# A two-layer trunk with mixture-of-experts on one core: two more experts in the fixed order, the order product and the id reads moved, the layer ends reordered

## The chip, the cores and the metric

One core of a Trainium2 chip runs the whole program. The metric is the device time of one execution in microseconds (us). All data are float32 unless a line says bf16. The profile is one execution taken by the hardware profiler; its times count from the start of its span.

## The reference, cut to what matters

Two layers work on 256 tokens (128 of a context pass, 128 of a denoising step) with 1024 columns. Each layer is a mixer followed by a mixture of experts; the change touches the mixture and the two places behind it.

```python
def hier_moe(h, w_rg, b_rg, w_re, b_re, w_g, w_u, w_d):      # h: tokens x 1024
    g_prob = softmax(x @ w_rg + b_rg)                        # 4 groups
    p_group, g_idx = top_k(g_prob, 1)
    e_in = the 8 expert logits of the chosen group
    top_p, top_i = top_k(softmax(e_in), 2)                   # 2 of 32 experts per token
    wts = top_p / sum(top_p) * p_group
    hid = silu(x @ w_g[e]) * (x @ w_u[e])                    # w_g, w_u: 1024 x 256 each
    y   = sum over e of gate[e] * (hid @ w_d[e])             # w_d: 256 x 1024
```

After each mixture `x = x + g2 * y`; after layer 0 the next mixer begins with a root mean square norm of `x`, after layer 1 the final norm `rms_norm(x, final_norm)` is the output. An expert has three matrices of 1 MiB, so the 32 experts of a layer are 96 MiB, and each of them is read once per layer. For the inputs given, the reference's routing sends these numbers of tokens to the experts that the kernel treats as fixed: layer 0, experts 0 to 7: 15, 22, 29, 16, 12, 7, 11, 24; layer 1: 31, 12, 18, 24, 12, 32, 10, 23. The four largest of the other 24 are 34, 34, 26, 23 in layer 0 and 71, 45, 44, 35 in layer 1.

## The kernel before, in words

**Routing.** `moe(l)` on each engine makes the router's logits, the masks and, by products with a triangle, the place of each token within its expert (`pos`) and the gates (`gat`). The experts 0 to 5 (`NFIX = 6`) are handled in a fixed order; the other 26 are ranked by how many tokens they have, so that an expert with many tokens gets many places. `order_by_count` on VectorE computes the ranks, and `order_tables` on TensorE turns them into ids with a small product (the order product, line L1319). VectorE's `ordered` writes the ids as integers into `route_i` (L2435) and SyncE reads them into registers.

**Passes.** The mixture runs in 11 passes, q = 0 to 10 (`PASSES`). Each pass fills the 128 columns of one tile of tokens: a pair has two experts with 64 places each, a quad four with 32, mono one with 128, and "three" one with 64 and two with 32. Pass by pass TensorE does: the up products (gate and up matrices of the pass, L1343, or by halves of the 1024 rows, L1357), the scatter of the pass before (L1400), transposes (`turn`), the gather of the next pass's tokens in two halves (L1333), the down products (L1389). ScalarE and VectorE copy the halves of the gather into `xg` (semaphores `m_xg1`, `m_xg0`) and apply the activation. In the last pass the down products and the scatter are cut in two (`last_down`, L1371, and `scatter_last`, L1407).

**Weights.** SyncE issues all weight transfers in one order into 11 slots of 2 MiB (`RING + MORE`). An up slot holds gate and up of one expert (or, by halves, half the rows of two experts); a down slot holds the down matrices of two experts, or of one alone where the pass has an odd number. A pass takes `slots_of(q)` slots: n for the ups and (n + 1) // 2 for the downs. Numbered in the order of the stream, slot p of a layer reuses the place of slot p - 11, and `slot_free(c)` waits on the semaphore `used` until TensorE has finished with that one (for the first slots of a layer with chunks of the work ahead: slots 9 and 10 come free by the modulation chunks 10 and 11 that `moe(l)` works through, L860). The ups of a pass give their slots back when the up products are done (by halves: half by half), the downs when the down products are. SyncE waits for the ids before pass 3, reads all ids of a pass and then issues its transfers:

```python
if q == NFIX // 2:
    sp.wait_ge(S.v_pos, 3 * l + 3)
```

**Layer ends.** After the last pass TensorE scatters the second half once VectorE's `weighted_rows` has written it (L2469). Then each engine reads the number of overflow rounds (`moe_further`; with more tokens than places an expert gets further rounds) and branches; the else side is empty. VectorE then adds the result to `xT` in four blocks (`add_scaled`, L2348) and, after layer 1, multiplies by the final gain into `hT` (L2614). ScalarE squares each block. After layer 1 TensorE transposes the first half into rows (`rows_out(0)`, L1558), sums the squares (L1566), and transposes the second half; the two row halves are scaled and stored.

Of the kernel before, what the change touches and what calls it, by code (L numbers as in the profile page):

```python
# [27 lines left out]
NB = 2  # L28
# [16 lines left out]
NFIX = 6  # L45
# [21 lines left out]
TILES = ([(NRANK + e, j) for e in range(NFIX) for j in range(2)] + [(r, j) for r in range(RANK4) for j in range(4)]  # L67
         + [(r, j) for r in range(RANK4, RANK2) for j in range(2)] + [(r, 0) for r in range(RANK2, NRANK)])
SHARE = {"mono": [0], "pair": [0, 1], "three": [0, 0, 1, 2], "quad": [0, 1, 2, 3]}
# [248 lines left out]
def build(nc, I, O):  # L318
    ctx = ExitStack()
    with ctx:  # L320
# [119 lines left out]
        sqo = part(4096, (KT, T))  # L440
# [63 lines left out]
        sqf = part(14100, (KT, T))  # L504
# [154 lines left out]
        def _(sp):  # L659
# [40 lines left out]
            def moe_layer(l):  # L700
                for q in range(NPASS):
                    c = moe_at[l] + PASS_AT[q]
                    if q == NFIX // 2:
                        sp.wait_ge(S.v_pos, 3 * l + 3)
                    ids = []
                    for kind, e in PASSES[q][1]:
                        if kind == "r":
                            e = sp.value_load(route_i[0:1, l, 9 + e:10 + e], min_val=0, max_val=NE - 1)
                        ids.append(e)
                    if by_halves(q):  # L710
# [5 lines left out]
                    else:  # L716
                        for e in ids:
                            expert_up(l, c, e)
                            c += 1
# [104 lines left out]
        def _(pe):  # L824
# [522 lines left out]
            def up_by_halves(share, c, between=None):  # L1347
# [63 lines left out]
            def moe_experts(l):  # L1411
# [4 lines left out]
                gather(1, 0, S.m_gat)  # L1416
                order_tables(l)
# [1257 lines left out]
```

## Time and profile before

| | |
|---|---|
| time of the kernel, median of 3 runs | 843.94 us (842.47 to 844.89) |
| the profiled execution's own time | 846.4 us |
| its span | 844.6 us |
| TensorE busy | 789.3 us, 93% of the span |
| VectorE, ScalarE busy | 321.8 us, 166.8 us |
| mean granted TensorE clock | 0.973 |
| moved by DMA | 291.47 MB, mean 345 GB/s |

The busy share of TensorE is an average over stages with different limits; the rate of the DMA over time says more here. The two mixtures lie at about 279 to 496 us (layer 0) and 616 to 832 us (layer 1).

### The profile page before, as it was taken

What the parts mean: (1) busy time and instruction counts of PE and PEld (TensorE: products, weight loads), DVE (VectorE), ACT (ScalarE), POOL (GpSimd) and SP (SyncE); (2) the same over time, 40 slices, a digit from 0 to 9 for tenths busy, and PEclk for the clock granted to TensorE, in tenths of its full rate; (3) what the DMA queues carried; (4) which work ended last, traced back from release to release, by engine and by line L of the source; (5) the groups of instructions that cost most, each with busy time, mean ns of one, the idle gap of its engine ahead of it and who ended that gap; (6) DMA issues with size and microseconds to landing.
All of it is one profiled execution on the core that took longest, in us unless ns stands there. A gap on an engine that the chain in (4) does not pass through costs nothing.

```text
span 844.6 us, 15977 instructions
## 1 busy us (share of the span) xinstructions
PE 789.3 (93%) x6913; PEld 525.5 (62%) x6913; DVE 321.8 (38%) x687; ACT 166.8 (20%) x323; POOL 12.3 (1%) x17
## 2 busy tenths in 40 slices
PE   3999999998999999999986989989999999999787
PEld 3788568677798665456542444779865555644335
DVE  1155467653414433433332340241543443333224
ACT  3112411323203111111110141130311111111012
POOL 0000001020000000000000000000000000000000
PEclk9999999999999999999998999999999999999898
DMA  9999779493899299999999999996549999999991
GB/s 342 387 371 386 260 261 349 147 345 108 270 393 395 111 417 410 402 416 415 420 414 412 401 386 385 388 409 269 199 168 416 407 398 417 415 421 416 410 398 70
DMA packets 97879, 291.47 MB, mean 345 GB/s; under 512 B 11833, under 2 KB 14991, under 8 KB 87567
## 3 DMA queue, kind: packets, MB, share of 16 engines
q1 hardware_dynamic: 86960, 284.32, 86.5%
q10 hardware_dynamic: 10847, 6.11, 2.5%
q8 instruction: 56, 0.92, 0.4%
q14 instruction: 16, 0.13, 0.0%
HBM read 288.30 MB, written 2.10 MB: 344 GB/s over the span
## 4 chain that ended last, share of the span: by engine, by line
PE 70%; SPq 11%; DMA 11%; ACT 3%; DVE 3%; issue 2%; ACTq 1%; DVEq 0%
PE psum L1357 7%; PE psum L1264 7%; PE psum L907 7%; PE psum L1343 5%; PE psum L1333 5%; PE psum L967 5%; DMA ring<-in_w_exp_up 5%; DMA scratch<-in_w_exp_up 5%; PE psum L860 5%; SPq L744 5%; PE psum L1389 4%; PE psum L1515 3%; PE psum L1528 3%; PE psum L1400 3%; SPq L733 2%
## 5 line engine op out<-in xcount | busy, mean ns | idle before, releaser
L1343 PE MATMUL psum<-scratch,hT 128*32 128x512 f32 (+1 forms) x384 | 79.5, 659 | 15.1 <-DMA ring<-in_w_exp_up 8.6
L1333 PE MATMUL psum<-scratch 128*128 128x128 f32 x704 | 84.0, 279 | 0.9 <-DVE scratch L2460 0.9
L1333 PEld LDWEIGHTS psum<-scratch 128*128 128x128 f32 x704 | 82.0, 195 | 1.2 <-issue 1.2
L1343 PE MATMUL psum<-ring,hT 128*32 128x512 f32 (+1 forms) x288 | 69.9, 641 | 2.5 <-DMA scratch<-in_w_exp_up 2.5
L907 PE MATMUL psum<-hT,ring 128*128 128x256 f32 x256 | 57.8, 382 | 1.1 <-DVE hT L2051 0.7
L1400 PEld LDWEIGHTS psum<-const,scratch 128*128 128x128 bf16 x480 | 45.1, 97 | 21.5 <-issue 13.6
L1400 PE MATMUL psum<-const,scratch 128*128 128x256 bf16 x480 | 55.9, 272 | 1.5 <-DVE scratch L2476 1.5
L2469 DVE TENSOR_SCALAR hT<-psum,const 128x512 f32<-128x512 f32 x22 | 16.5, 751 | 106.3 <-PE psum L1389 93.6
L1343 PEld LDWEIGHTS psum<-scratch,hT 128*32 128x32 f32 (+1 forms) x384 | 21.4, 123 | 54.5 <-issue 54.5
L907 PEld LDWEIGHTS psum<-hT,ring 128*128 128x128 f32 x256 | 47.8, 190 | 9.6 <-DVE hT L2051 2.0
L1885 ACT ACTIVATE scratch<-psum 128x256 f32<-128x256 f32 x22 | 8.5, 384 | 210.0 <-PE psum L1343 123.2
L1357 PE MATMUL psum<-scratch,hT 128*64 128x512 f32 (+1 forms) x208 | 42.7, 593 | 0.3 <-DMA scratch<-in_w_exp_up 0.3
L967 PE MATMUL psum<-ring,hT 128*128 128x512 f32 x96 | 42.6, 596 | 0.0
L860 PE MATMUL psum<-ring,condT 128*2 128x128 f32 x1280 | 40.1, 280 | 1.0 <-issue 1.0
L2480 DVE TENSOR_TENSOR scratch<-psum,scratch 128x256 f32<-128x256 f32 x22 | 9.3, 425 | 83.0 <-ACT scratch L1885 82.9
L1389 PE MATMUL psum<-scratch,const 128*32 128x512 f32 (+2 forms) x248 | 40.1, 596 | 0.0
L860 PEld LDWEIGHTS psum<-ring,condT 128*2 128x2 f32 x1280 | 32.2, 87 | 8.5 <-issue 5.3
L1357 PE MATMUL psum<-ring,hT 128*64 128x512 f32 (+1 forms) x176 | 35.7, 594 | 1.3 <-DMA ring<-in_w_exp_up 1.3
L1343 PEld LDWEIGHTS psum<-ring,hT 128*32 128x32 f32 (+1 forms) x288 | 18.2, 121 | 27.5 <-issue 27.5
L1389 PE MATMUL psum<-ring,const 128*32 128x512 f32 (+2 forms) x216 | 32.8, 596 | 0.0
L967 PEld LDWEIGHTS psum<-ring,hT 128*128 128x128 f32 x96 | 17.8, 190 | 20.8 <-issue 20.8
L1264 PEld LDWEIGHTS psum<-hT,ring 128*128 128x128 f32 x256 | 28.8, 192 | 0.7 <-issue 0.7
(334 smaller groups left out, 1032.8 us busy)
## 6 DMA issues: line engine op xcount, KB each, us to landing
ring<-in_w_mod SPq DMA_DIRECT2D x40, 1024.0 KB, 11.4
scratch<-in_w_exp_down SPq DMA_DIRECT2D x28, 1024.0 KB, 16.2
ring<-in_w_exp_down SPq DMA_DIRECT2D x24, 1024.0 KB, 17.4
scratch<-in_w_exp_gate SPq DMA_DIRECT2D x22, 1024.0 KB, 16.8
scratch<-in_w_exp_up SPq DMA_DIRECT2D x22, 1024.0 KB, 18.4
ring<-in_w_exp_gate SPq DMA_DIRECT2D x18, 1024.0 KB, 15.5
ring<-in_w_exp_up SPq DMA_DIRECT2D x18, 1024.0 KB, 18.2
scratch<-in_w_exp_gate SPq DMA_DIRECT2D x26, 512.0 KB, 11.0
```

The source lines that it names most:

```text
L744: sp.dma_start(slot(s)[:, at:at + 1024], w[e][:, 1024 * kh:1024 * kh + 1024]).then_inc(full[s], 16)
L860: last = mm(bank[mbank[g]][32 * m:32 * m + NB, at:at + P], condT[:, :, k], w[:, k, m * P:(m + 1) * P], start=(k == 0), stop=(k == KT - 1))
L907: last = mm(out[:, c2 * T:(c2 + 1) * T], w[:, k, m * P:(m + 1) * P], hT[:, k, :, :], start=(k == 0 and k1 == KT), stop=(k == k1 - 1), skip ...
L967: last = mm(bank[b], hT[:, k, t, :], w[:, k, :], start=(k == 0), stop=(k == KT - 1))
L1264: last = mm(bank[2 * t + m // 4][:, (m % 4) * P:(m % 4 + 1) * P], w[m // 4][:, k, (m % 4) * P:(m % 4 + 1) * P], hT[:, k, t, :], start=(k = ...
L1333: last = mm(bank[b][:, k * P:(k + 1) * P], hrow[:, t, half * 4 + k, :], Pm[:, t, :], start=(t == 0), stop=(t == 1))
L1343: last = mm(bank[0][i * m:(i + 1) * m, :], xg[:, k, i * m:(i + 1) * m], w[e][:, k, :, :], start=(k == 0), stop=(k == KT - 1))
L1357: last = mm(bank[0][i * m:(i + 1) * m, :], xg[:, 4 * kh + k, i * m:(i + 1) * m], w[i // 2][:, i % 2, k, :, :], start=(kh == 0 and k == 0), ...
L1389: last = mm(bank[1 + half][i * m:(i + 1) * m, :], hidT[:, a, i * m:(i + 1) * m], slot(slots[e // 2])[:, base:base + 512], start=(a == 0), ...
L1400: last = mm(bank[4 + k // 2][:, (k % 2) * T:(k % 2 + 1) * T], y3[:, j, k, :], ohT, start=False, stop=True, skip_group_check=True)
L1515: last = mm(bank[4 + 2 * j + t], hT[:, k, t, :], w[:, k, :], start=(k == 0), stop=(k == KT - 1))
L1528: last = mm(bank[b][:, (m % 2) * T:(m % 2 + 1) * T], w[:, k, m * P:(m + 1) * P], hT[:, k, :, :], start=(k == 0), stop=(k == KT - 1))
```

## The change

1. Passes: `NFIX` goes from 6 to 8. Experts 6 and 7 get 32 places each and share a new pass 3, a "three", with the expert of rank 3 (64 places). The quads move back; the last pass stays a quad of ranks.
2. SyncE waits for the ids at the first ranked expert of pass 3 only, which is now that pass's third, and reads each id just before that expert's transfer (passes that are not by halves).
3. TensorE: the order product stands between the two halves of the first gather; the second half goes to bank 4 instead of bank 0; the four transposes of `pos` and `gat` follow it (`rows_of_tables`), with a count of their own on `t_pos`. VectorE's `ordered` goes ahead of `weighted`. The first pass's up products wait only for the half of `xg` that they read.
4. Layer ends: `scatter_last(1)`, `weighted_rows` and the additions move into both sides of the branch. On the else side the first block is added before `weighted_rows`; after layer 1 the sums of squares are made block by block (`square_sums`), the first ahead of `scatter_last(1)`, and the final gains of the first half go to a place of their own (`finl`). The squares of layer 0's end go to `sqm` as well.

```diff
-NFIX = 6
+NFIX = 8
+NPAIR = 3
...
-          ("quad", [("r", 6 + i) for i in range(4)], 24), ("pair", [("r", 1), ("r", 2)], 16),
-          ("quad", [("r", 10 + i) for i in range(4)], 28), ("mono", [("r", 0)], 12),
-          ("quad", [("r", 14 + i) for i in range(4)], 32), ("quad", [("r", 18 + i) for i in range(4)], 36),
-          ("three", [("r", 3), ("r", 4), ("r", 5)], 20), ("quad", [("r", 22 + i) for i in range(4)], 40)]
+          ("three", [("e", 6), ("e", 7), ("r", 3)], 20), ("quad", [("r", 4 + i) for i in range(4)], 24),
+          ("pair", [("r", 1), ("r", 2)], 16), ("quad", [("r", 8 + i) for i in range(4)], 28), ("mono", [("r", 0)], 12),
+          ("quad", [("r", 12 + i) for i in range(4)], 32), ("quad", [("r", 16 + i) for i in range(4)], 36),
+          ("quad", [("r", 20 + i) for i in range(4)], 40)]
...
-SHARE = {"mono": [0], "pair": [0, 1], "three": [0, 0, 1, 2], "quad": [0, 1, 2, 3]}
+SHARE = {"mono": [0], "pair": [0, 1], "three": [0, 1, 2, 2], "quad": [0, 1, 2, 3]}
...
             def moe_layer(l):
                 for q in range(NPASS):
                     c = moe_at[l] + PASS_AT[q]
-                    if q == NFIX // 2:
-                        sp.wait_ge(S.v_pos, 3 * l + 3)
                     ids = []
                     for kind, e in PASSES[q][1]:
                         if kind == "r":
+                            if q == NPAIR:
+                                sp.wait_ge(S.v_pos, 3 * l + 3)
                             e = sp.value_load(route_i[0:1, l, 9 + e:10 + e], min_val=0, max_val=NE - 1)
                         ids.append(e)
+                        if not by_halves(q):
+                            expert_up(l, c, e)
+                            c += 1
...
-            def order_tables(l):
+            def rows_of_tables(l):
 
                 for n, v in enumerate((pos, gat)):
                     for t in range(NB):
-                        nc.tensor.transpose(bank[1][0:NE, (2 * n + t) * P:(2 * n + t + 1) * P], v[:, t, 0:NE], ident)
+                        last = nc.tensor.transpose(bank[1][0:NE, (2 * n + t) * P:(2 * n + t + 1) * P], v[:, t, 0:NE], ident)
+                last.then_inc(S.t_pos, 1)
+
+            def order_tables(l):
+
                 pe.wait_ge(S.v_pos, 3 * l + 2)
...
                 for kh in range(2):
+                    pe.wait_ge([S.m_xg0, S.m_xg1][kh], n_pass + 1)
                     for u in range(c + n * kh, c + n * kh + n):
                         slot_full(pe, u)
...
                 pe.wait_ge(S.v_pos, 3 * l + 1)
-                gather(1, 0, S.m_gat)
                 order_tables(l)
+                gather(1, 4, S.m_gat)
+                rows_of_tables(l)
...
-                        idle_products(3, 3)
-                        pe.wait_ge(S.m_yr1, n + 1)
-                        scatter_last(1).then_inc(S.t_fin, 1)
...
+            def square_sums(b):
+
+                pe.wait_ge(S.a_sq, SQ0[5] + b + 1)
+                for k in (2 * b, 2 * b + 1):
+                    for t in range(NB):
+                        last = mm(bank[t][:, 0:1], sqm[:, k, t * P:(t + 1) * P], ones[:, 0:1],
+                                  start=(k == 0), stop=(k == KT - 1), skip_group_check=True)
+                return last
...
                 with pe.Else():
-                    pe.nop()
+                    if l == DEPTH - 1:
+                        square_sums(0)
+                    else:
+                        idle_products(3, 3)
+                    pe.wait_ge(S.m_yr1, (l + 1) * NPASS)
+                    scatter_last(1).then_inc(S.t_fin, 1)
...
+            square_sums(1)
             rows_out(0)
-            for k in range(KT):
-                if k % 2 == 0:
-                    pe.wait_ge(S.a_sq, SQ0[5] + k // 2 + 1)
-                for t in range(NB):
-                    last = mm(bank[t][:, 0:1], sqf[:, k, t * P:(t + 1) * P], ones[:, 0:1],
-                              start=(k == 0), stop=(k == KT - 1), skip_group_check=True)
-            last.then_inc(S.t_ms, 1)
+            square_sums(2)
+            square_sums(3).then_inc(S.t_ms, 1)
             rows_out(1)
...
                         V.tensor_copy(xg[:, 0:4, :], heads(bank[3])).then_inc(S.m_xg0, 1)
+                        ordered(l)
                         weighted(gat[:, :, 0:2], 2).then_inc(S.m_p, 1)
-                        ordered(l)
                         overflow(l)
...
                 with dve.Else():
-                    dve.nop()
-
-                for b in range(4):
-                    dve.wait_ge(S.t_fin, 2 * l + 1 + b // 2)
-                    add_scaled(bank[4 + b], b, l * MT + 5 * KT).then_inc(S.v_y, 1)
+                    add_experts(l, 0)
+                    dve.wait_ge(S.used, done)
+                    weighted_rows().then_inc(S.m_yr1, 1)
+                    add_experts(l, 1)
                     if l == DEPTH - 1:
...
+                        final_weights(0)
+                        final_weights(1)
+                    add_experts(l, 2)
+                    add_experts(l, 3)
+                    if l == DEPTH - 1:
+                        final_weights(2)
+                        final_weights(3)
```

## Rows read from the trace of the kernel before

**Rows 1.** The page's GB/s of DMA, in 40 slices of 21.1 us.
```profile
GB/s 342 387 371 386 260 261 349 147 345 108 270 393 395 111 417 410 402 416 415 420 414 412 401 386 385 388 409 269 199 168 416 407 398 417 415 421 416 410 398 70
```
**Rows 2.** Windows: stretch, its length, TensorE's clock, DMA busy share, GB/s.
```profile
273.70:290.10 16.40, 0.90 0.06 15
290.10:345.40 55.30, 1.00 1.01 412
345.40:346.60 1.20, 1.00 0.78 212
346.60:480.20 133.60, 0.96 1.02 414
...
601.00:625.00 24.00, 0.93 0.24 89
...
681.80:816.10 134.30, 0.96 1.02 414
```
**Rows 3.** Waits of SyncE's queue, 280 to 500 us: total, times, longest.
```profile
SPq L708 <- DVE route_i L2435: 22.9, 1, 22.9
```
**Rows 4.** Timeline of SyncE's issues, layer 0: start, us, line, transfer, count.
```profile
262.08 0.89 SPq L763 DMA_DIRECT2D ring<-in_w_exp_down  x2
288.54 0.37 SPq L733 DMA_DIRECT2D ring<-in_w_exp_gate  x1
...
345.05 0.33 SPq L733 DMA_DIRECT2D ring<-in_w_exp_gate  x1
```
**Rows 5.** Pieces of the chain that ended last: start, us, what.
```profile
273.06 3.91 PE psum L860 x127
...
279.36 5.44 PE psum L1333 x32
285.70 7.02 PE psum L1357 x32
...
302.50 6.87 PE psum L1357 x32
...
337.85 7.00 PE psum L1343 x64
...
426.70 8.80 PE psum L1343 x64
```
**Rows 6.** Timeline of VectorE: the ids of layer 0 are written.
```profile
285.74 0.17 DVE L2435 CAST route_i<-psum 1x26 int32<-1x26 f32 x1 [2.60 <-PE psum L1320]
```
**Rows 7.** TensorE timeline: up products behind a wait (in brackets, with its releaser).
```profile
452.17 1.06 PE L1343 MATMUL psum<-scratch,hT 128*32 128x512 f32 x2 [6.39 <-DMA ring<-in_w_exp_up]
...
480.39 3.64 PE L1357 MATMUL psum<-scratch,hT 128*32 128x512 f32 x32 [0.26 <-DMA scratch<-in_w_exp_up]
...
816.25 3.64 PE L1357 MATMUL psum<-ring,hT 128*32 128x512 f32 x32 [1.30 <-DMA ring<-in_w_exp_up]
```
**Rows 8.** TensorE windows: length, busy (instructions), granted clock, DMA share, GB/s.
```profile
424.30:426.70 2.40, 0.00 (x0) 1.00 0.99 401
...
427.20:430.40 3.20, 3.20 (x21) 0.51 1.03 410
...
837.00:838.00 1.00, 1.00 (x6) 0.50 0.00 0
```
**Rows 9.** Timeline of VectorE and TensorE at the two layer ends.
```profile
494.07 4.23 DVE L2348 SCALAR_TENSOR_TENSOR xT<-psum,modT,xT 128x128 f32<-128x128 f32 x16
...
829.05 0.75 DVE L2469 TENSOR_SCALAR hT<-psum,const 128x512 f32<-128x512 f32 x1 [6.37 <-PE psum L1371]
829.91 1.13 DVE L2348 SCALAR_TENSOR_TENSOR xT<-psum,modT,xT 128x128 f32<-128x128 f32 x4
831.07 0.62 DVE L2614 TENSOR_SCALAR hT<-xT,cols 128x256 f32<-128x256 f32 x2
...
834.36 4.53 PE L1566 MATMUL psum<-const,scratch 128*128 128x1 f32 x32
...
834.98 1.12 DVE L2348 SCALAR_TENSOR_TENSOR xT<-psum,modT,xT 128x128 f32<-128x128 f32 x4
```

More of the change, by code:

```diff
@@ L439, in build @@
         vtk = part(2048, (NB, D))
-        sqo = part(4096, (KT, T))
         vsq = part(6144, (D,))
@@ L503, in build @@
         yrow = part(12000, (NB, D))
-        sqf = part(14100, (KT, T))
+        finl = part(2304, (4, NB, P))
         ab = small[:, 0:32]
@@ L715, in moe_layer @@
                                 c += 1
[L716 to L719, printed above, removed]
                     if q == NPASS - 1:
@@ L1345, in experts_up, with up_by_halves @@
                 last.then_inc(sem, n)
-            def up_by_halves(share, c, between=None):
+            def up_by_halves(share, c, n_pass, between=None):
                 n = len(share) // 2
@@ L1557, in rows_out @@
                     for k in range(4):
[L1558 removed]
+                        last = nc.tensor.transpose(bank[2 + 2 * t + half][:, k * P:(k + 1) * P],
+                                                   finl[:, k, t, :] if half == 0 else hT[:, 4 + k, t, :], ident)
                     last.then_inc(S.t_last, 1)
+            square_sums(1)
             rows_out(0)
[L1562 to L1568 removed]
+            square_sums(2)
+            square_sums(3).then_inc(S.t_ms, 1)
             rows_out(1)
@@ L1935, in _ @@
             roots()
[L1936 removed]
+            stream_squares(3, sqm)
             norm(3, 1, 1, 0)
@@ L2563, in moe_experts @@
                         V.tensor_copy(xg[:, 0:4, :], heads(bank[3])).then_inc(S.m_xg0, 1)
-                    dve.wait_ge(S.used, c + sum(slots_of(q)))
                     if more:
+                        dve.wait_ge(S.used, c + sum(slots_of(q)))
                         weighted_rows().then_inc(S.m_v, 1)
@@ L2604, in moe_further @@
                     dve.wait_ge(f.f_end, 1)
+                    for b in range(4):
+                        add_experts(l, b)
+                    if l == DEPTH - 1:
+                        for b in range(4):
+                            final_weights(b)
                 with dve.Else():
-                    dve.nop()
-                for b in range(4):
-                    dve.wait_ge(S.t_fin, 2 * l + 1 + b // 2)
-                    add_scaled(bank[4 + b], b, l * MT + 5 * KT).then_inc(S.v_y, 1)
+                    add_experts(l, 0)
+                    dve.wait_ge(S.used, done)
+                    weighted_rows().then_inc(S.m_yr1, 1)
+                    add_experts(l, 1)
                     if l == DEPTH - 1:
-                        dve.wait_ge(S.v_y, 4 * l + b + 1)
-                        for k in (2 * b, 2 * b + 1):
-                            last = V.tensor_scalar(hT[:, k, :, :].rearrange("p t n -> p (t n)"), xT[:, k, :, :].rearrange("p t n -> p (t n)"),
-                                                   cols[:, V_FIN + k:V_FIN + k + 1], None, ALU.mult)
-                        if b % 2 == 1:
-                            last.then_inc(S.v_last, 1)
+                        final_weights(0)
+                        final_weights(1)
+                    add_experts(l, 2)
+                    add_experts(l, 3)
+                    if l == DEPTH - 1:
+                        final_weights(2)
+                        final_weights(3)
             moe(0)
```

46 lines of the change are left out of this document (30 added, 16 removed).

## The prediction

> **What bounds the kernel now.** I read the page's DMA rate first, since 93% of busy TensorE is a mean over unlike stages. The rate is near 400 to 420 GB/s through both mixtures and falls to 111 GB/s in the slice at their start in layer 0 (the fourteenth number) and to 199 and 168 before layer 1's (the twenty-ninth and thirtieth) [rows 1]. The windows put edges on this: in layer 0 the DMA does nothing from 273.7 to 290.1 us, then it is full until 345.4, dips for about a microsecond, and is full again until 480.2 and beyond; layer 1 shows the same shape [rows 2]. The waits say why it stops: SyncE stands 22.9 us at the ids [rows 3]. Its last issue before is at 262.08, and its first after is at 288.54 [rows 4], 2.6 us behind the end of the write of the ids at 285.91 [rows 6]: four id reads, some 0.65 us each. From that issue to the first bytes at 290.1 [rows 2] pass 1.6 us.
>
> Then come the TensorE rows. Up to 426 us the chain is TensorE alone; pass 0 starts its ups at 285.7, pass 1 at 302.5, pass 3 at 337.85 [rows 5]. The ups of the later passes wait for weights: 6.39 us in pass 9, 0.26 us and 1.30 us for the second half of pass 10 in layer 0 and layer 1 [rows 7]. So the mixture begins as TensorE's and ends as the DMA's. What counts for its end is how much is still to be loaded when the DMA goes full for good, and that moment is the dip at 345.4 to 346.6.
>
> The dip is the heart of the case. At 345.05 SyncE issues an up transfer [rows 4], just after the ups of pass 3 end at 337.85 + 7.00 = 344.85 [rows 5]. It is slot 20, which takes the place of slot 9, the first up of pass 3. The slots, not the ids, hold the DMA back at this point. The account by hand agrees: nine slots (18 MiB) were there at 290.1, and 55.3 us at 412 GB/s are 22.8 MB or 21.7 MiB, so 39.7 MiB; slots 0 to 19 of the old order hold 18 (three pairs) + 12 (quad) + 6 (pair) + 4 (two ups) = 40 MiB.
>
> **The change, part by part.**
>
> *Fixed experts and the new pass 3.* Slots 9 and 10 now take experts 6 and 7 without ids. They come free when modulation chunks 10 and 11 are used, at about 275.0 and 277.0 us (halves of the L860 piece that ends at 276.97 [rows 5]). With 1.6 us to the first bytes and 5.06 us per slot of 2 MiB (2.53 us per MiB, from 1.049 MB at 414 GB/s [rows 2]), the DMA is empty again at 286.7. So of the 16.4 us gap 10 us are filled. But now all 11 slots are full, and slot 11 (rank 3) needs pass 0's first up half, used at 285.7 + 3.5 = 289.2. It flows from 290.9. I walked on with the same prices. Slot 12 holds the downs of experts 6 and 7; slot 13 waits for pass 0's downs at 302.5 and holds only 1 MiB, since the third expert's down is alone in it: empty from 301.0 to 304.1, full to 306.6. Slots 14 and 15 wait for pass 1's halves (306.0, 309.4), slot 16 for its downs (about 320.7), slot 19 for pass 2's downs (337.85), so that slot 19 is loaded at about 344.6. Slot 20 again waits for pass 3's ups at 344.85 and flows from 346.5.
>
> So both kernels stand at the same gate at the same time, and the question is only what is left. Slots 0 to 19 of the new order hold 18 + 9 (three) + 12 (quad) = 39 MiB against 40. Left are 57 MiB against 56. Behind the gate no later slot is short in either (slots 20 to 22 are 6 MiB or 15 us of transfer, and slot 23 comes free at about 355.5, one pass of 17.7 us, half of 302.5 to 337.85, after 337.85). The DMA's end moves by 1 MiB, **+2.5 us a layer, +5.1 us in all**. Does the end follow? The waits of 0.26 and 1.30 us for the last ups say that TensorE has no slack there [rows 7]; pass 9 is now a quad, its ups wait as before, and behind them lie 12 MiB instead of 11 before the last up half. Bounds: 4.6 (TensorE's own pace hides some) to 5.6 us.
>
> *Clock.* The added 2.5 us of waiting falls mostly ahead of the last up half, where TensorE idled 0.26 and 1.30 us. After an idle of 2.4 us at 424.3 the granted clock was 0.51 for 3.2 us, the 1.2 GHz level [rows 8], and those ups took 8.80 us instead of 7.00 [rows 5]. Behind the last up half lies a stretch that is TensorE's to the end. So +1.8 us for each layer in which the clock falls, between 0 and 3.6. From two layers with even odds I take one: **+1.8 us**. The Trainium skill, TensorE: Matmul & The Clock Gate, under HAM oscillation — how this bites in real kernels, tells of a thin kernel in which each DMA wait sends the array back to the half clock and the next products start cold; here the trace agrees at 427.2 us [rows 8], and taken as a rule for both waits it would give the 3.6.
>
> *Order product, ids, first half.* The ids come about 2.9 us sooner (gather's second half, half of 5.44 us [rows 5], and the transposes no longer stand ahead), and one read instead of four precedes a transfer. Both gain nothing now: slot 11 waits for TensorE until 289.2, later than the ids even before (285.9 [rows 6]). If slots were free these would be worth 2.9 + 2.0 us a layer. TensorE's own order has the same instructions between 279.4 and 285.7 [rows 5], so pass 0 starts where it did: nothing, bounds -0.2 to +0.3, since the first up half waited for nothing before. `ordered` ahead of `weighted` delays the latter by 0.2 us, and it is not needed until the turn behind the ups (292.7). The later copy of `pgrow` on ScalarE is needed at 292.7 too. Thirty-two places hold the 11 and 24, 10 and 23 tokens of experts 6 and 7, and the largest ranks fit, so no further rounds.
>
> *End of layer 0.* VectorE's additions run from 494.07 to 498.30 [rows 9]. The first block moves ahead of `weighted_rows`, the third then waits for the scatter's end, 2 us behind its start at 494.0, and two blocks of 1.06 follow, so they end at about 498.2: -0.1 us.
>
> *End of layer 1.* Now: `weighted_rows` 829.05 to 829.80, then add and gain in turn, the fourth addition ends at 836.1, its square at 836.8, and TensorE's sums run 834.36 to 838.89, the last at half clock [rows 8, 9]. New: the first block is done ahead of 829.05, the second runs 829.9 to 831.0, gains of two blocks (4 x 0.31) to 832.3, third 832.3 to 833.4 (the second scatter half is over by then), fourth to 834.6, its square 835.3, its sum (a quarter of 32 instructions, 0.8 us at full clock) 836.1. The roots follow 2.8 us sooner than at 838.89, the last rows are ready sooner by as much. **-2.8 us**; -1.5 if the clock falls there again or the branch, now followed by critical work, costs a microsecond; -3.3 at best. The cover of the first sums is the wait for `weighted_rows`; if it fails they cost 0.8.
>
> **Sum:** 5.1 + 1.8 - 0.1 - 2.8 = +4.0 us. On the profiled execution: span 844.6 to 848.6, own time 846.4 to 850.4; on the median of the runs, 843.94, it gives **847.9 us**.
>
> **Rivals.**
> *(a) The end is the DMA's, one MiB later a layer, as above*: 0.79. Inside it: no clock fall in either last half, +2.2 us, 846.1 (0.25); one fall, 847.9 (0.33); two, 849.7 (0.21).
> *(b) The filled gap counts* (0.09). If some place were free sooner than I read, so that the DMA is full from 290.9 on with 22 MiB in hand rather than from 290.1 with 18, 4 MiB or 10 us a layer less, less 0.8 for the later start: 843.94 - 18.6 - 2.9 = 822 us. For it: 10 us more of transfer ahead of pass 0. Against it: SyncE's issue at 345.05 stands at a slot, not at an id. It decides from the point at which the DMA no longer empties between 301 and 346 us. The Trainium skill, Trainium Kernel Development and Optimization, under Best Practices, asks to overlap DMA with compute, and the new fixed loads do just that; by this rule alone the change should gain, by the slots it cannot.
> *(c) TensorE hides the extra MiB* (0.12): if the last up half waits by less than the rows say, only the ends count, 843.94 - 2.9 = 841.0 us. Against it: waits on weights in both layers.
>
> **Numbers.** Uncertainty of a measurement here is about 0.3%, 2.5 us. Faster than 841.4: (b) and part of (c), 0.14. Within: the rest of (c) and most of the case without clock falls, 0.29. Slower than 846.5: 0.57. The range 842.5 to 851.5 holds (a) with its bounds (4.6 to 5.6, 0 to 3.6, -1.5 to -3.3) and leaves out (b) and most of (c).
>
> **What would show it.** Right: DMA windows of the new trace with no long gap at 274 to 290 but with several short ones up to 346, full from there; the last up half of pass 10 some 2.5 us later in layer 0 and about 5 in layer 1, waiting for weights; 7.0 us instead of 9.8 from the start of `weighted_rows` in layer 1 (829.05) to the end of the sums of squares (838.89) [rows 9]. Wrong: a DMA that stays full from 291, or ups of pass 9 that start at the old times.

## The result and the profile after

The changed kernel takes 856.38 us (median of 5 runs, 851.16 to 857.01) against 844.89 us (842.47 to 846.39) for the kernel before, run in turns with it: a ratio of 1.0124, 95% interval 1.0098 to 1.0149, or 8 to 13 us more. The forecast was 847.9 us and slower; the direction is right, and the size is missed by 8.5 us, with the measured time outside the range that ended at 851.5. The profiled execution took 856.92 us with a span of 854.9 us, 10.3 us longer than the span before. TensorE is busy for 785.4 us, 4 us less than before, and so idle for some 14 us more. That doesn't mean that all of the loss is waiting: some work got slower and some got faster, as the pieces below show.

The page's GB/s of the changed kernel, in 40 slices of 21.4 us, answers to [rows 1].

```profile
GB/s 344 386 370 386 252 262 335 162 344 102 297 411 327 363 267 360 350 417 418 414 422 408 398 387 385 392 410 184 198 337 303 324 334 420 415 417 419 411 401 108
```

The empty slice 14 of before (111) is gone; there are now five thin ones instead (327 363 267 360 350). SyncE's issues in layer 0 say where each stop is: start, us, line, transfer, count.

```profile
275.69 0.34 SPq L733 DMA_DIRECT2D ring<-in_w_exp_gate  x1
...
277.44 0.33 SPq L733 DMA_DIRECT2D ring<-in_w_exp_gate  x1
...
288.45 0.36 SPq L733 DMA_DIRECT2D scratch<-in_w_exp_gate  x1
...
301.51 0.89 SPq L766 DMA_DIRECT2D scratch<-in_w_exp_down  x2
...
344.02 0.35 SPq L744 DMA_DIRECT2D ring<-in_w_exp_gate  x1
```

This is the walk through the slots that the prediction made by hand. Experts 6 and 7 go out at 275.69 and 277.44 without ids (forecast 275.0 and 277.0), the third expert at 288.45 when pass 0's first half gives its place (forecast 289.2), the lone down transfer at 301.51 (302.5), and slot 20 at 344.02, just behind the ups of pass 3. In the kernel before slot 20 went out at 345.05 [rows 4]. Now the windows around it: stretch, length, TensorE's busy time and instructions, its granted clock, DMA busy share, GB/s. The first fence is layer 0, and the second is layer 1.

```profile
276.90:286.80 9.90, 8.96 (x86) 1.00 0.95 394
286.80:290.00 3.20, 3.20 (x18) 1.00 0.39 100
...
300.00:303.00 3.00, 3.00 (x16) 1.00 0.24 71
303.00:343.80 40.80, 40.80 (x279) 1.00 0.85 333
343.80:345.80 2.00, 2.00 (x22) 1.00 0.36 74
345.80:347.00 1.20, 1.20 (x13) 1.00 0.95 297
347.00:349.00 2.00, 2.00 (x20) 1.00 0.89 234
349.00:351.00 2.00, 2.00 (x22) 1.00 0.98 383
351.00:360.00 9.00, 9.00 (x92) 1.00 1.02 401
360.00:483.00 123.00, 106.49 (x827) 0.96 1.02 415
```

```profile
689.70:691.00 1.30, 1.30 (x15) 1.00 0.90 290
691.00:693.00 2.00, 2.00 (x21) 1.00 1.02 317
693.00:695.00 2.00, 2.00 (x22) 1.00 1.02 242
695.00:700.00 5.00, 5.00 (x52) 1.00 1.00 352
```

The reader is to see two things. The gap of 16.4 us [rows 2] has become several short ones, all ahead of 346 us. And behind the gate, where before the rate was at 414 GB/s at once [rows 2], the DMA engines are busy from 346 us on but move 234 to 297 GB/s for some 3 us in layer 0, and 242 to 352 GB/s for some 10 us in layer 1. The prediction priced that stretch at the full rate.

Next is the chain of work that ended last in the changed kernel: start, us, what. The second fence has three pieces of the kernel before.

```profile
284.66 7.02 PE psum L1362 x32
...
336.81 7.00 PE psum L1347 x64
...
482.97 5.29 PE psum L1362 x32
...
508.85 15.67 PE psum L1538 x32
...
570.75 5.47 PE psum L1565 x32
...
680.74 7.00 PE psum L1347 x64
...
828.30 5.00 PE psum L1362 x32
```

```profile
504.19 13.97 PE psum L1515 x32
...
564.40 3.84 PE psum L1542 x32
...
673.07 7.00 PE psum L1343 x64
```

From these pieces the 10.3 us can be split, since between them both kernels do the same work:

| stretch | before | after | difference |
|---|---|---|---|
| start to the first up products, layer 0 | 285.70 | 284.66 | -1.0 |
| end of pass 3's ups (344.85, 343.81) to the last up half, layer 0 | 135.54 | 139.16 | +3.6 |
| the same, layer 1 (680.07, 687.74) | 136.18 | 140.56 | +4.4 |
| last up half itself, both layers | 3.67, 3.67 | 5.29, 5.00 | +3.0 |
| layer 1's mixer, the pieces at 508.85 and 570.75 | 13.97, 3.84 | 15.67, 5.47 | +3.3 |
| end of the last up half, layer 0, to layer 1's mixer | 20.13 | 20.59 | +0.5 |
| end of the last up half, layer 1, to the first output transfer (840.24, 850.59) | 20.32 | 17.29 | -3.0 |
| all else | | | -0.5 |

The windows on the four longer pieces show why they are longer: the granted clock is at the lower of its two levels, 1.2 GHz, for the 3 us that each window spans.

```profile
483.00:486.00 3.00, 3.00 (x16) 0.50 1.05 386
510.20:513.20 3.00, 3.00 (x5) 0.50 1.06 388
571.80:574.80 3.00, 3.00 (x16) 0.50 1.02 408
828.00:831.00 3.00, 2.70 (x16) 0.50 1.05 386
```

TensorE's timeline shows what stood before three of them. The second line is a stop at the end of layer 0, which the last sections come back to. Columns: start, us, line, operation, count, and in brackets the idle time before it and its releaser.

```profile
482.97 5.25 PE L1362 MATMUL psum<-scratch,hT 128*32 128x512 f32 x32 [3.08 <-DMA scratch<-in_w_exp_up]
...
502.70 2.10 PE L880 MATMUL psum<-scratch,const 128*128 128x256 f32 x9 [1.00 <-issue]
...
508.85 6.66 PE L1538 MATMUL psum<-ring,hT 128*128 128x512 f32 x11 [2.18 <-ACT hT L1632]
...
828.30 4.96 PE L1362 MATMUL psum<-ring,hT 128*32 128x512 f32 x32 [3.12 <-DMA ring<-in_w_exp_up]
```

The waits for the last up weights have grown from 0.26 and 1.30 us [rows 7] to 3.08 and 3.12 us. The end of layer 1 answers to [rows 9]; VectorE's `weighted_rows` and TensorE's last sums of squares:

```profile
842.43 0.75 DVE L2489 TENSOR_SCALAR hT<-psum,const 128x512 f32<-128x512 f32 x1 [0.76 <-PE psum L1376]
...
847.16 2.08 PE L1482 MATMUL psum<-const,scratch 128*128 128x1 f32 x16 [0.16 <-ACT scratch L1627]
```

From 842.43 to 849.24 are 6.8 us, where before it was 9.8 [rows 9]. That part did what the prediction said (7.0).

### The profile page after: what moved, and what is told of

The parts are those of the page before. It is cut to its first block, busy times and chain, and to the rows that moved or that the text cites. A ratio compares the mean times of both kernels' runs of the same rounds, so it can differ in the third digit from the quotient of the medians.

```text
span 854.9 us, 15953 instructions
## 1 busy us (share of the span) xinstructions
PE 785.4 (92%) x6910; PEld 523.2 (61%) x6910; DVE 321.6 (38%) x687; ACT 166.6 (19%) x323; POOL 12.3 (1%) x17
## 4 chain that ended last, share of the span: by engine, by line
PE 80%; SPq 8%; DMA 4%; DVE 2%; ACT 2%; issue 2%; ACTq 1%; DVEq 0%
PE psum L1347 8%; PE psum L1362 8%; PE psum L1337 8%; PE psum L1264 7%; PE psum L907 7%; PE psum L1394 7%; PE psum L860 5%; PE psum L967 5%; SPq L744 5%; PE psum L1405 4%; PE psum L1538 3%; SPq L763 3%; PE psum L1551 3%; PE psum L1029 2%; DMA ring<-in_w_exp_up 2%; DMA scratch<-in_w_exp_up 2%
## 5 line engine op out<-in xcount | busy, mean ns | idle before, releaser
L1347 PE MATMUL psum<-ring,hT 128*32 128x512 f32 (+1 forms) x304 | 73.7, 610 | 12.9 <-DMA scratch<-in_w_exp_up 12.9
L1347 PE MATMUL psum<-scratch,hT 128*32 128x512 f32 (+1 forms) x368 | 73.8, 616 | 11.9 <-DMA ring<-in_w_exp_up 11.9
L907 PEld LDWEIGHTS psum<-hT,ring 128*128 128x128 f32 x256 | 47.8, 190 | 9.6 <-DVE hT L2071 2.0
L1362 PE MATMUL psum<-scratch,hT 128*64 128x512 f32 (+1 forms) x192 | 40.8, 630 | 5.1 <-DMA scratch<-in_w_exp_up 3.1
L1362 PE MATMUL psum<-ring,hT 128*64 128x512 f32 (+1 forms) x192 | 40.5, 624 | 4.6 <-DMA ring<-in_w_exp_up 3.1
L1394 PE MATMUL psum<-scratch,const 128*32 128x512 f32 (+2 forms) x264 | 43.7, 596 | 0.0
L967 PE MATMUL psum<-ring,hT 128*128 128x512 f32 x96 | 42.6, 597 | 0.0
L1538 PE MATMUL psum<-ring,hT 128*128 128x512 f32 x64 | 29.7, 624 | 2.2 <-ACT hT L1632 2.2
```

The source lines that it names most:

```text
L907: last = mm(out[:, c2 * T:(c2 + 1) * T], w[:, k, m * P:(m + 1) * P], hT[:, k, :, :], start=(k == 0 and k1 == KT), stop=(k == k1 - 1), skip ...
L967: last = mm(bank[b], hT[:, k, t, :], w[:, k, :], start=(k == 0), stop=(k == KT - 1))
L1347: last = mm(bank[0][i * m:(i + 1) * m, :], xg[:, k, i * m:(i + 1) * m], w[e][:, k, :, :], start=(k == 0), stop=(k == KT - 1))
L1362: last = mm(bank[0][i * m:(i + 1) * m, :], xg[:, 4 * kh + k, i * m:(i + 1) * m], w[i // 2][:, i % 2, k, :, :], start=(kh == 0 and k == 0), ...
L1394: last = mm(bank[1 + half][i * m:(i + 1) * m, :], hidT[:, a, i * m:(i + 1) * m], slot(slots[e // 2])[:, base:base + 512], start=(a == 0), ...
L1538: last = mm(bank[4 + 2 * j + t], hT[:, k, t, :], w[:, k, :], start=(k == 0), stop=(k == KT - 1))
```

## The experiments

Each kernel was timed in turns with the kernel before, in three sets; that kernel gave 845.4, 845.4 and 845.5 us in them. The changed kernel was not in these sets, so a difference from its 856.38 us is one between medians of two sets. "Gate to last half" is the stretch of the table above, 135.5 and 136.2 us before, 139.2 and 140.6 us after.

### Which part costs: the passes alone, the passes back, the ends alone

**e1_passes_only** is the kernel before with the new passes, their tiles, and SyncE's wait and id reads.

```diff
-NFIX = 6
+NFIX = 8
+NPAIR = 3
...
-                    if q == NFIX // 2:
-                        sp.wait_ge(S.v_pos, 3 * l + 3)
...
+                            if q == NPAIR:
+                                sp.wait_ge(S.v_pos, 3 * l + 3)
```

> The kernel before with the new passes, their places and SyncE's id reads, and nothing else of the change. If the pass order is the cost (one MiB more left at slot 20's gate, a slow restart, clock falls behind longer waits): 10 to 14 us over the kernel before, since the changed kernel's gain at its end (3 us) is missing, so 856 to 859 us. If the cost lies in the order product, the first half or the layer ends: within 2.5 us of before. The order product is late again here, and should cost nothing, since slot 11 waits for TensorE at 289 us anyway.

Measured 858.19 us (855.33 to 858.98), 1.0152 [1.0127, 1.0178]. The passes alone cost as much as the whole change. Gate to last half is 139.7 and 141.8 us. The last up halves take 5.09 us behind a wait of 3.07 us in layer 0, and 3.67 us behind a wait of 3.13 us in layer 1. The profiled execution is the fastest of the five (855.33 us, mean granted clock 0.975; the other four have 0.967 or 0.968), so its trace shows less clock loss than this kernel usually has.

**e2_passes_back** is the changed kernel with the passes of before (`NFIX = 6`, the old `PASSES`, `TILES` and `SHARE`); the order product, the id reads and the layer ends stay changed.

> The changed kernel with the passes of before and six fixed experts; ids one by one, order product, first half and layer ends stay. If the passes carry the cost: 3 to 7 us faster than before (3 from the end of layer 1, and up to 2 x 2 from SyncE's issue at the start of the mixture about 5 us sooner, since here slots 9 and 10 are free and the ids are what it waits for), so 837 to 842 us. If the slot gate at pass 3 cancels an earlier start in this order too, only the end's 3 us: 841 to 842. If another part carries the cost: over 850.

Measured 845.17 us (841.24 to 849.24), 1.0001 [0.9979, 1.0023], above what was expected. Earlier ids alone gain nothing: the slots hold the stream back anyway.

**e3_ends_only** is the kernel before with part 4 of the change alone.

```diff
-                for b in range(4):
-                    dve.wait_ge(S.t_fin, 2 * l + 1 + b // 2)
-                    add_scaled(bank[4 + b], b, l * MT + 5 * KT).then_inc(S.v_y, 1)
+                    add_experts(l, 0)
+                    dve.wait_ge(S.used, done)
+                    weighted_rows().then_inc(S.m_yr1, 1)
+                    add_experts(l, 1)
```

> The kernel before with the layer ends of the change alone. If the reading of the two last stretches is right: 2.5 to 3.5 us faster than before, 841 to 842 us. If the branch with critical work behind it costs as much as it hides: no difference.

Measured 843.79 us (841.89 to 847.46), 0.9983 [0.9966, 0.9999]: 1.5 us gained, where 3 were expected. The end of layer 1 gives its 3.0 us in this trace too (20.96 us to the first output transfer, 23.99 before, both from the start of the last up half, where the table counts from its end), and the end of layer 0 its 0.1. But in the mixer of layer 1 this kernel shows the same two longer pieces as the changed one. Chain of e3_ends_only:

```profile
501.16 15.67 PE psum L1530 x32
...
563.07 5.47 PE psum L1557 x32
```

In front of the second of them TensorE waits equally long in this kernel and in the kernel before. TensorE's timeline, first the kernel before, then e3_ends_only:

```profile
564.40 1.83 PE L1542 MATMUL psum<-scratch 128*128 128x128 f32 x14 [2.16 <-ACT scratch L1962]
```

```profile
563.07 3.17 PE L1557 MATMUL psum<-scratch 128*128 128x128 f32 x16 [2.16 <-ACT scratch L1974]
```

The same idle of 2.16 us is followed by the full clock in one and by 0.54 of it in the other. In front of the first piece the wait did grow, from 0.92 to 2.18 us, because TensorE is done with the earlier products sooner and ScalarE's `hT` is not. The chains of all thirteen kernels, one execution each, say how far the two longer pieces go with the new ends:

| kernels | ends | longer mixer pieces |
|---|---|---|
| before, e1_passes_only, e11_before_full | old | none |
| after, e3_ends_only, e6_full_rows, e7_idle_last | new | both |
| e2_passes_back | new | the first |
| e4_quad_third, e9_quad_full, e10_ten_full | new | the second |
| e5_mono_fourth, e8_ten_passes | new | none |

The waits are the same in all ten kernels with the new ends (2.18 or 2.19 us, and 2.16 us). So the 3.3 us are a fall of the clock that happens in some executions and not in others; it was seen with the new ends only, but two kernels with them are without it, and three traces without them are few. That the new ends cause it isn't shown.

### Is it the order of the stream, or the half rows?

**e4_quad_third** keeps experts 6 and 7 fixed and early, but in a quad with ranks 6 and 7, so that pass 3 takes 12 MiB as before; rank 3 goes back to the late "three".

```diff
-          ("three", [("e", 6), ("e", 7), ("r", 3)], 20), ("quad", [("r", 4 + i) for i in range(4)], 24),
+          ("quad", [("e", 6), ("e", 7), ("r", 6), ("r", 7)], 24), ("pair", [("r", 1), ("r", 2)], 16),
...
```

> The changed kernel, but experts 6 and 7 sit in a quad with ranks 6 and 7 as pass 3, and the three stays late, so that the slots hold what they held before (40 MiB up to slot 19). If the one MiB and what follows from it is the cost: 8 to 12 us faster than the changed kernel and 2 to 4 faster than before, 840 to 843 us. If loading fixed experts early is itself the cost (11 full slots, an empty queue at each slot): within 3 us of the changed kernel.

Measured 844.68 us (842.35 to 848.2), 0.9996 [0.9975, 1.0017], 11.7 us less than the changed kernel. Gate to last half is 135.4 and 136.8 us. Filling the gap at 274 us is thus neither a loss nor a gain; the loss is gone with 40 MiB ahead of the gate and no half rows right behind it, and this run doesn't tell one from the other.

**e5_mono_fourth** puts the mono pass (rank 0) right behind the new pass 3, so that a quad's transfers stand at the gate and the half rows come behind them; slots 0 to 19 then hold 38 MiB instead of 39.

```diff
-          ("three", [("e", 6), ("e", 7), ("r", 3)], 20), ("quad", [("r", 4 + i) for i in range(4)], 24),
+          ("three", [("e", 6), ("e", 7), ("r", 3)], 20), ("mono", [("r", 0)], 12), ("quad", [("r", 4 + i) for i in range(4)], 24),
```

> The changed kernel with the mono pass moved from place 7 to place 4, right behind the new pass 3. Its two slots hold 3 MiB, so slots 0 to 19 hold 38 MiB instead of 39. Gate account: another MiB, 2.5 us, a layer is left behind the gate, or up to 5 if a short mono pass also empties the DMA again: 5 to 8 us over the changed kernel, 861 to 865 us. If not the bytes ahead of the gate but the early loads as such are the cost: no difference from the changed kernel, 855 to 857.

Measured 857.11 us (854.49 to 861.35), 1.0151 [1.0123, 1.018]: no different from the changed kernel, where the gate account wanted 861 to 865 us. Gate to last half is 140.8 and 141.4 us, 1.7 and 0.9 us more than there, where one more MiB behind the gate should cost 2.5. The windows behind the gate, e5_mono_fourth, layer 0:

```profile
345.00:347.00 2.00, 2.00 (x20) 1.00 0.89 252
347.00:349.00 2.00, 2.00 (x20) 1.00 1.04 420
```

The stream is at its full rate 3 us after the gate here. So this run changes two things at once: it leaves one more MiB behind the gate than the changed kernel, and it loses the slow restart. Against the kernel before it leaves 2 MiB more, 5.1 us at 2.53 us each, and its stretches are 5.3 and 5.2 us longer.

**e6_full_rows** is the changed kernel with the up transfers of pass 5 (the pair of ranks 1 and 2, slots 20 and 21) by whole experts instead of by half rows.

```diff
-            return PASSES[q][0] == "pair" or q == NPASS - 1
+            return (PASSES[q][0] == "pair" and q != 5) or q == NPASS - 1
```

> The changed kernel, but pass 5 (the pair of ranks 1 and 2, whose ups are the first transfers behind the gate) loads and multiplies its ups whole instead of by halves: rows of 8 KiB in place of 4 KiB. If the slow 5 to 8 us behind the gate (225 to 300 GB/s at a full busy share) come from the half rows issued into an empty queue: 1.5 to 4 us faster than the changed kernel, 852 to 855. If the restart is slow whatever the rows are: no difference.

Measured 849.47 us (847.88 to 852.78), 1.0052 [1.0029, 1.0075]: 6.9 us less than the changed kernel, more than either side expected; 1.0124 and 1.0052 are ratios whose intervals are apart. The windows behind the gate, e6_full_rows, layer 0:

```profile
345.00:347.00 2.00, 2.00 (x21) 1.00 0.76 201
347.00:349.00 2.00, 2.00 (x21) 1.00 1.01 414
```

The rate is full at once. Gate to last half falls to 137.5 and 137.5 us, and the two last up halves take 3.67 us each, with no clock fall, though TensorE waited about as long ahead of them. In the two traces the stretches account for 4.7 us of the difference and the last up halves for 3.0, and the second part is the clock's and may be luck:

```profile
481.67 3.64 PE L1362 MATMUL psum<-scratch,hT 128*32 128x512 f32 x32 [3.12 <-DMA scratch<-in_w_exp_up]
...
822.34 3.64 PE L1362 MATMUL psum<-ring,hT 128*32 128x512 f32 x32 [2.83 <-DMA ring<-in_w_exp_up]
```

**e7_idle_last** tries to hold the clock: eight small zero products ahead of the wait for the last up half.

```diff
+                        idle_products(3, 8)
```

> The changed kernel with eight more products on zeros between the scatter and the last up half of pass 10, in the time in which TensorE waits for weights. If the clock fall in that wait costs what the trace shows (1.3 to 1.6 us in each layer): 1 to 3 us faster than the changed kernel, 853.5 to 855.5, with no granted clock of 0.5 behind the last up half's start. If the fall hits work that waits for weights anyway: no difference.

Measured 856.88 us (855.77 to 863.78), 1.0144 [1.0112, 1.0175]: no difference. In its trace the products shorten the idle to 1.23 and 1.26 us, and the last up halves still take 5.1 us. That execution was the slowest of its six (863.78 us), and it has a stop of 2.69 us at the end of layer 0.

### Do half rows cost everywhere?

A view of the DMA in two stretches in which half rows run: 346.5 to 349 us of the changed kernel, behind the gate, and 312 to 320 us of the kernel before, behind other transfers (rows of 4 KiB in both). The columns are the queue, packets, MB, and their time as a share of 16 engines. Changed kernel:

```profile
q1 hardware_dynamic: 167, 0.61, 92.4%
```

Kernel before:

```profile
q1 hardware_dynamic: 841, 3.24, 101.8%
```

That is 0.61 / 2.5 = 244 GB/s and 3.24 / 8 = 405 GB/s. Packets of about one size took 0.924 x 16 x 2.5 / 167 = 221 ns behind the gate and 1.018 x 16 x 8 / 841 = 155 ns in full flow. Two hypotheses were then put to three kernels. By theory A half rows are slow only when they start into an empty queue, and that costs time only behind the slot that binds. By theory B they cost their time wherever they stand.

**e9_quad_full** is e4_quad_third with pass 4's pair by whole experts. In e4_quad_third the half rows of slot 16 start into an empty queue at 318.5 us, 24 us ahead of the gate.

```diff
-            return PASSES[q][0] == "pair" or q == NPASS - 1
+            return (PASSES[q][0] == "pair" and q != 4) or q == NPASS - 1
```

> The kernel of the quad in pass 3, with the up transfers of pass 4's pair (ranks 1 and 2) by whole experts instead of by half rows. In that kernel the half rows start into an empty queue at 318.5 us and the windows 320 to 322 and 322 to 324 show 233 and 223 GB/s at a full busy share. Theory A (half rows into an empty queue are slow, but what counts is only what is lost behind the binding slot, whose up transfer is issued at 342.75): those windows rise to about 410 GB/s, the time does not move, 844 to 846 us. Theory B (each slow stretch costs its time, wherever it stands): about 1.8 us a layer less, 841 us.

Measured 843.4 us (841.47 to 846.62), 0.9975 [0.9955, 0.9995]; e4_quad_third had 0.9996 [0.9975, 1.0017]. Windows of e4_quad_third, with half rows, and of e9_quad_full, without:

```profile
318.00:320.00 2.00, 2.00 (x12) 1.00 0.22 53
320.00:322.00 2.00, 2.00 (x12) 1.00 1.02 233
322.00:324.00 2.00, 2.00 (x12) 1.00 0.97 223
```

```profile
320.00:322.00 2.00, 2.00 (x12) 1.00 0.04 16
322.00:324.00 2.00, 2.00 (x12) 1.00 0.85 283
324.00:326.00 2.00, 2.00 (x12) 1.00 1.03 434
```

The whole trace of e9_quad_full lies 2.6 us later, so that its window from 320 us stands beside the other's from 318. The slow stretch of 4 us at a full busy share shows again with half rows, and not without them. The intervals of the two kernels overlap; a gain of 1.8 us a layer is excluded by neither, but the stretch from the gate to the last half in layer 0 is the same, 135.2 against 135.4 us. In layer 1 it is 135.2 against 136.8, 1.6 us less, about what theory B wants.

**e10_ten_full** is e8_ten_passes (below) with whole experts for its pair in pass 3, whose half rows are issued behind transfers that still run.

> The kernel of ten passes, with the up transfers of pass 3's pair by whole experts. There the half rows are issued at 301.8 us behind transfers that still run, and the windows 300 to 310 show 409 to 413 GB/s. Theory A (only an empty queue makes half rows slow): no difference, 823 to 828 us, the packets alone are longer. Theory B (half rows are dearer everywhere, by some per cent of 4 MiB a layer): 1 to 3 us faster.

Measured 825.42 us (823.06 to 826.67), 0.9763 [0.9733, 0.9793], against 825.22 us for e8_ten_passes: no difference.

**e11_before_full** is the kernel before with whole experts for its pair in pass 4, where the queue is full.

> The kernel before, with the up transfers of pass 4's pair by whole experts. Its half rows stand in a full queue (406 GB/s from 310 to 325 us). Theory A: 844 to 846 us, no difference. Theory B: 1 to 3 us faster. By whole experts the slots of the pair come free both at the end of its ups instead of one half way, which could cost up to 3.4 us of prefetch a layer if the slot of pass 7 behind them were the binding one; slot 20 binds, so nothing is expected of that.

Measured 847.02 us (845.26 to 850.97), 1.0025 [1.0004, 1.0045]: no gain, perhaps a small loss, within what these runs can tell from no change. Half rows behind running transfers cost nothing that these runs can see; into an empty queue they run at 223 to 317 GB/s. Whether a slow stretch ahead of the slot that binds costs time is open: layer 0 of e9_quad_full says no, layer 1 says yes, and the two medians are too close to decide.

### A version by the same account

**e8_ten_passes** puts experts 0 to 3 into one quad of 32 places, its ups by halves, as pass 0, so that the mixture has ten passes; pass 2 is the quad of experts 6 and 7 with ranks 6 and 7, and the third fixed "three" is gone.

```diff
-NPAIR = 3
+NPAIR = 2
...
-PASSES = [("pair", [("e", 0), ("e", 1)], 0), ("pair", [("e", 2), ("e", 3)], 4), ("pair", [("e", 4), ("e", 5)], 8),
-          ("three", [("e", 6), ("e", 7), ("r", 3)], 20), ("quad", [("r", 4 + i) for i in range(4)], 24),
+PASSES = [("quad", [("e", i) for i in range(4)], 0), ("pair", [("e", 4), ("e", 5)], 4),
+          ("quad", [("e", 6), ("e", 7), ("r", 6), ("r", 7)], 20), ("pair", [("r", 1), ("r", 2)], 12),
...
```

> Everything of the changed kernel but its passes: experts 0 to 3 as one quad of 32 places by halves, 4 and 5 a pair, 6 and 7 with ranks 6 and 7 a quad, then pair, quad, mono, quad, quad, three, quad: ten passes and the same 96 MiB and 49 slots. Same transfers ahead of the ids (22 MiB), but the first pass gives back six slots instead of three and the third is done a pass earlier. By the gate account, walked on with the same prices, the DMA is full from about 287 on but for 3 us, and the end of each mixture comes 10 us sooner than before: 822 to 828 us. If the mixture's end hung on something else than the slots given back early (TensorE's pace, or early loads): within 5 us of the fourth run, 840 to 850 us.

Measured 825.22 us (823.07 to 828.35), 0.9762 [0.9735, 0.9789]: 20 us faster than the kernel before, 31 us faster than the changed one. Its windows at the start of the mixture, layer 0; its half rows start in the second:

```profile
290.00:300.00 10.00, 9.43 (x86) 1.00 0.97 394
300.00:310.00 10.00, 10.00 (x57) 1.00 1.02 410
```

With four experts used up in pass 0 it gives back six slots instead of three, and the stream runs without a further stop from 290 us instead of 346. TensorE is busy for 752.9 us instead of 789.3, one pass a layer less, and no run separates the two. That the stream's part counts shows at the end of the mixture: the last up half starts at 470.69 us instead of 480.39, and TensorE still waits 2.47 us for its weights ahead of it (2.23 us in layer 1), so with weights that arrive as before a shorter TensorE would only have waited longer there. The quad gives experts 0 to 3 the 32 places that their 15, 22, 29, 16 and 31, 12, 18, 24 tokens need here; with other routing, more than 32 tokens on one of them would take further rounds.

## Why the prediction was right in sign and wrong in size

**Right.** The slots, not the ids, hold the stream: the walk's times of issue came out within about a microsecond, e2_passes_back gained nothing from earlier ids, and e4_quad_third nothing from the filled gap. So rival (b), the filled gap counts, and rival (c), TensorE hides the MiB, both fell: the last up halves wait 3.08 and 3.12 us. The ends gave -3.0 us in layer 1 (forecast -2.8). The prediction read the first bytes at 290.1 us, 1.6 us behind the issue at 288.54. That is where the rate is near its full value: a window from 289.4 to 289.8 already has 205 GB/s. The walk needs the later time, so its sum stands.

The first up products start 1.0 us sooner, but not by the moved order product: e1_passes_only, without it, has them at 284.38 us. In the kernel before, the gather of layer 0 ran partly at the lower clock (5.44 us for 32 products [rows 5]; after, the two halves take 2.02 and 1.98 us). Nor is this one microsecond the change's: e11_before_full, which is the same up to there, has them at 283.99 us, with 5.44 us for the gather.

**Wrong: the term "1 MiB = 2.5 us a layer, +5.1 us in all".** It measured 3.6 + 4.4 = 8.0 us. The failed step is "Behind the gate no later slot is short in either", taken together with the price of 2.53 us per MiB: it priced every MiB behind the gate at 414 GB/s and did not look at which transfers stand there. In the new order they are the half rows of ranks 1 and 2, and they start into an empty queue. What the windows miss against 414 GB/s is, in layer 0, 117 x 1.2 + 180 x 2 + 31 x 2 + 13 x 9 = 680 KB or 1.6 us, and in layer 1, 124 x 1.3 + 97 x 2 + 172 x 2 + 62 x 5 = 1010 KB or 2.4 us. With the 2.5 us of the MiB that makes 4.1 and 4.9 us, against 3.6 and 4.4 measured. Two runs without half rows at the gate bear this out. In e6_full_rows the MiB costs 2.0 and 1.3 us, less than the forecast and below its lower bound of 4.6 in all. In e5_mono_fourth two MiB cost 5.3 and 5.2 us, against 5.1 at the forecast's price. So the price per MiB was right in one and too high in the other, and what the term lacked is the slow restart.

**Wrong: the term "Clock, +1.8 us".** This term missed by more than the first: 6.3 us against 1.8. It put even odds on each of the two last up halves, and both fell (3.0 us, inside the bound of 3.6). That both did is the luck of this execution: of the eight last up halves behind waits of 2.8 to 3.2 us, two each in the changed kernel, e1_passes_only, e5_mono_fourth and e6_full_rows, three were slow. And the term left out every other place in which the clock can fall: two more falls lie in the mixer of layer 1, 3.3 us, which the prediction put at nothing without a reason. They don't come from the passes alone, since e3_ends_only has both without the new passes; whether the new ends bring them is open, since e5_mono_fourth and e8_ten_passes have the new ends and neither fall. The clock is not a matter of the profiled execution alone: the mean granted clock is 0.968 to 0.972 in the five executions of the changed kernel, and 0.971 to 0.981 in 29 of the kernel before.

The Trainium skill, TensorE: Matmul & The Clock Gate, under HAM oscillation — how this bites in real kernels, says that products behind a DMA wait start cold, and taken as a rule for both waits it gave 3.6. In the changed kernel the trace agrees; in e6_full_rows it doesn't, where waits of 3.12 and 2.83 us were followed by the full clock.

**Wrong by half a microsecond: the end of layer 0**, +0.5 instead of -0.1. TensorE's stream has a stop of 1.00 us with no releaser behind the branch. Before, it fell among products that nobody waited for, up to 501.35 us; now it lasts up to 502.70, inside the sums of squares that the next root needs. In e3_ends_only, e8_ten_passes and e10_ten_full, where no such stop shows, this stretch is 20.0 us, 0.1 less than before; in five other kernels with the new ends it stops there too (0.86 to 1.02 us), and the stretch is 20.5 to 20.6 us.

The sum, as measured on the profiled execution: 8.0 (passes) + 6.3 (clock) + 0.5 - 3.0 (ends) - 1.0 (first ups) - 0.5 (rest) = 10.3 us, against the forecast 5.1 + 1.8 - 0.1 - 2.8 = 4.0. Of the 6.3 us between them, 4.5 are the clock's and 2.9 those of the passes; the end of layer 0 adds 0.6, and the rest takes 1.7 off.

**What stays open.** Why a half-row transfer is slow only into an empty queue wasn't tried further. A half-row transfer is also half as large (512 KB against 1 MB), and no run separates the length of the rows from the size of the transfers; the packet times say that each packet takes longer, not what it waits for. Why the clock falls after one idle of 2.2 us and not after another is open as well, and with it whether the new ends, through the longer wait of 2.18 us, cost what they gain. The places of the clock falls are read from one execution of each kernel, and how much of the 11.5 us between the medians is theirs isn't known.

## What to carry to other kernels

With a ring of slots, count what is loaded ahead of the last slot that binds, and what is left behind it: here a gap filled ahead of it was worth nothing, and a MiB moved behind it cost 1.3 to 2.7 us a layer, where the full rate wants 2.5. Then look at which transfers restart the stream there, since a full busy share is not a full rate. If the ring binds, use up more weights per pass early on: with one pass a layer less, that was worth 20 us, where e4_quad_third, the reordering that keeps 40 MiB ahead of the gate, was worth nothing that can be told. Look at more than one execution before a clock fall is put down to a change. And when a part ends sooner, look for what now waits in its place before counting the gain.

## What the runs showed of the hardware

- Transfers of 4 KiB rows (half the rows of two experts) that start into an empty queue moved 223 to 317 GB/s at a DMA busy share of 0.89 to 1.02, with 221 ns a packet, against 155 ns and 405 GB/s behind running transfers. Rows of whole experts reached 414 GB/s in the same place.
- The same idle of 2.16 us at one place in the mixer was followed by the full clock in six kernels and by the lower one in seven. Waits of 3.07 and 3.13 us in one execution of e1_passes_only were followed by the lower and the full clock; 3.12 us by the full clock in e6_full_rows, and 1.23 us, with zero products ahead of it, by the lower clock (0.50) in e7_idle_last. The length of the last wait alone doesn't decide.
- A stop in TensorE's stream with no releaser lies at the end of layer 0, behind the branch: 1.00 us up to 501.35 in the kernel before, 1.00 up to 502.70 after, 0.74 up to 505.37 in e1_passes_only, 2.69 up to 505.57 in e7_idle_last, none to be seen in e3_ends_only, e8_ten_passes and e10_ten_full. Where it lay ahead of sums that the next root needs, it cost about half a microsecond.
